# The head of a compression stage: small loads, a retention step, a bias product and a row copy in other places

## What is computed

```python
def _compress(kv_rows, pe_k, w1_k, w2_k, pe_v, w1_v, w2_v, k_norm_g):
    ...
    def phi(x, pe, w1, w2):
        x = (x + pe[:, None, :]).transpose(0, 1, 3, 2, 4).reshape(B, n_cmp, NSA_GROUPS, CMP_BLK * HEAD_DIM)
        return jax.nn.gelu(x @ w1) @ w2

    kc = _rms(phi(blk[:, :, :, 0], pe_k, w1_k, w2_k), k_norm_g)
    vc = phi(blk[:, :, :, 1], pe_v, w1_v, w2_v)
...
def _ret_chunk(R, q, k, v):
    ...
    o = o + jnp.einsum('bnhd,bhde->bnhe', q, R) * xi[None, :, :, None]
    R = jnp.exp(C * lg)[None, :, None, None] * R + jnp.einsum('bmhd,bmhe->bhde', k * zeta[None, :, :, None], v)
    return o, R
...
        return win[:, QS:]            # the window of the sample: its old rows, moved up by 4, and the new ones
```

## Time and profile before

| | us |
|---|---|
| median of 3 runs | 2939.29 (2936.84 to 2944.8) |
| the profiled execution, its own time | 2942.77 |
| its span in the trace | 2941.1 |
| projection, until the barrier | 0 to 435.2 |
| TensorE in the compression | 435.3 to 670.7 |
| prompt's attention begins | 673.9 |
| first expert's product | 1400.2 |

### The profile page before, as it was taken

How to read it: one execution, slowest core, us unless ns; L and a number is a source line. 1 busy time by engine, 2 the same in 40 slices (tenths; PEclk the granted TensorE clock), 3 DMA queues, 4 the chain that set the end, 5 groups by cost and what they waited for, 6 DMA issues and landing times.

```text
span 2941.1 us, 44519 instructions
## 1 busy us (share of the span) xinstructions
PE 2695.6 (92%) x18178; PEld 2223.1 (76%) x18178; DVE 945.1 (32%) x2675; ACT 636.7 (22%) x1613; POOL 484.7 (16%) x465
## 2 busy tenths in 40 slices
PE   7999976998998758993999999999999999999995
PEld 3555435545665557451999999999999999999994
DVE  1222222216766412345222232323232232223221
ACT  1111211115765400121011111111111111111111
POOL 0000011101000000022032131313132232122221
PEclk9999985998999856996999999999999999999997
DMA  5000036203000121222778788888898999999995
GB/s 187 11 22 20 23 116 142 58 1 113 2 1 1 58 86 58 94 81 95 284 231 275 260 263 275 278 291 292 308 302 303 331 320 308 331 315 312 317 327 166
DMA packets 276770, 533.64 MB, mean 181 GB/s; under 512 B 51906, under 2 KB 88226, under 8 KB 276354
## 3 DMA queue, kind: packets, MB, share of 16 engines
q1 hardware_dynamic: 223842, 472.66, 45.1%
q0 software_dynamic: 33312, 46.98, 7.5%
q10 hardware_dynamic: 19408, 11.10, 1.4%
HBM read 492.21 MB, written 42.96 MB: 182 GB/s over the span
## 4 chain that ended last, share of the span: by engine, by line
PE 51%; DMA 1%; DVE 1%; SPq 0%; POOL 0%; issue 0%; POOLq 0%; DVEq 0%; ACT 0%; ACTq 0%
PE up L2047 34%; PE down L2058 17%; DMA w_up<-summed_rows 1%; DMA slot_rows<-slot_tokens_gates 0%; DMA summed_rows<-y_rows,row_index_cur 0%; SPq L1995 0%; POOL summed_rows L2011 0%; PE down L2064 0%; POOLq L1891 0%; DVE nb L2179 0%; DVE hT L2136 0%; DVEq L1956 0%; DVE obt L2185 0%; DVE obt L2190 0%; DVE osf L2191 0%
## 5 line engine op out<-in xcount | busy, mean ns | idle before, releaser
L2047 PE MATMUL up<-hT,w_up 128*128 128x128 f32 (+19 forms) x8192 | 1006.6, 286 | 18.2 <-DVE hT L2136 18.2
L2047 PEld LDWEIGHTS up<-hT,w_up 128*128 128x128 f32 x8192 | 1003.5, 191 | 18.5 <-issue 18.5
L2058 PE MATMUL down<-actT,w_down 128*128 128x128 f32 (+19 forms) x4096 | 507.8, 286 | 0.0
L2058 PEld LDWEIGHTS down<-actT,w_down 128*128 128x128 f32 x4096 | 503.6, 191 | 1.1
L2011 POOL DMA_INDIRECT summed_rows<-y_rows,row_index_cur x153 | 240.9, 1574 | 1084.2 <-ACT y_rows L2077 1047.6
L2156 DVE TENSOR_SCALAR glu<-up,b_up_cur 128x128 f32<-128x128 f32 (+19 forms) x256 | 93.7, 366 | 1012.6 <-PE up L2047 1012.6
L306 PE MATMUL zp<-w_in,xnT 128*128 128x512 f32 (+3 forms) x896 | 355.7, 553 | 1.4 <-DVE xnT L476 1.4
L306 PEld LDWEIGHTS zp<-w_in,xnT 128*128 128x128 f32 (+1 forms) x896 | 153.5, 187 | 178.4 <-issue 174.6
L2088 ACT ACTIVATE sig<-glu 128x128 f32<-128x128 f32 (+19 forms) x256 | 82.4, 322 | 867.1 <-DVE glu L2156 867.1
L2096 ACT ACTIVATE yT<-down,b_down_cur 128x128 f32<-128x128 f32 (+19 forms) x256 | 97.0, 379 | 394.6 <-PE down L2058 394.6
L2005 POOL DMA_INDIRECT x_rows<-h_rows,row_index_cur x153 | 149.6, 977 | 65.2 <-issue 46.0
(11 more groups left out here) (395 smaller groups left out, 2070.6 us busy)
## 6 DMA issues: line engine op xcount, KB each, us to landing
w_up<-in_w_up SPq DMA_DIRECT2D x128, 2048.0 KB, 12.7
w_down<-in_w_down SPq DMA_DIRECT2D x64, 2048.0 KB, 12.6
w_in<-in_w_in SPq DMA_DIRECT2D x5, 2048.0 KB, 13.1
cache_rows<-in_cache_slc_kv SPq DMA_DIRECT2D x40, 128.0 KB, 2.5
x<-in_x_prompt SPq DMA_DIRECT2D x8, 512.0 KB, 3.8
window_rows<-in_cache_win_kv SPq DMA_DIRECT2D x8, 512.0 KB, 4.3
window_rows<-in_x_prompt SPq DMA_DIRECT2D x8, 512.0 KB, 4.0
summed_rows<-rg SPq DMA_DIRECT2D x8, 512.0 KB, 2.6
```

The lines of the kernel that those rows point to most:

```text
L2047: mm = nc.tensor.matmul(up[c % 2][:, h, :N], U[c // 4][:, h, kk, w0:w0 + P], hT[:, kk, :N], start=(kk == 0), stop=(kk == KC - 1))
L2058: mm = nc.tensor.matmul(dn[d % 2][:, :N], Dn[:, kk // 4, kk % 4, d * P:d * P + P], aT[:, kk, :N], start=(kk == 0), stop=(kk == KC - 1))
```

## The change

Seven edits in the head of the compression:
1. The two encodings and the gain are loaded by SyncE in the projection, in step t = 2, into `k.key` and `k.cnt`, which are free until the experts.
2. w1 of the values is loaded by ScalarE's queue behind its 16 pages of group 1 instead of at the start.
3. The copy of the old window rows goes from the projection to the end of SyncE's queue in the prompt's attention, behind the cache loads; `nout` of the sample tile is 3 instead of 4.
4. The retention's operands lie elsewhere (`x2T0` and the PSUM tiles `ctp1`, `ctp2`, `kcp`, `vcp`), and T(0,1) follows T(0,0) at once. `sample_operands()` stands on VectorE behind the first copy of M(0,0).
5. `retention()` stands on TensorE inside M(0,0), between the hidden halves hh = 0 and hh = 1. T(1,0) waits until its outputs have been copied from `ctp`.
6. The bias product takes one column of encodings, repeated 32 times, as the stationary operand and 256 columns of w1 as the moving one: 16 products, the step jj in column group jj % 4 (32 of 128 columns), so that the 16 steps leave four partial sums on 128 partitions.
7. VectorE copies these partial sums into `ret_sq`, and two products by a column of 1/32 (L796 after the change) add them up into the bias, behind the half hh = 0.

```diff
@@ phase_project
-        nout = lambda t: (4 if t == PT else 1 if t > PT else 3 if t >= 4 else 2)
+        nout = lambda t: (1 if t > PT else 3 if t >= 4 else 2)
             for t in range(NA):
+                if t == 2:
+                    with nc.allow_non_contiguous_dma(reason="position encodings and gain, small"):
+                        for j, n in enumerate(("k", "v")):
+                            sp.dma_start(k.pe_c[:, j, :], i[f"cmp_pe_{n}"][0].rearrange("(c r) d -> (r d) c", r=2)).then_inc(k.s_enc, 16)
+                        for half in range(2):
+                            sp.dma_start(k.gkc[64 * half:64 * half + 64, :], i["k_norm_cmp_g"].rearrange("l d -> d l")).then_inc(k.s_enc, 16)
...
-                    sp.dma_start(ws[:, :WIN - QS, :], i["cache_win_kv"].rearrange("l b s k g d -> (l b) s (k g d)")[:, QS:, :]).then_inc(so, 16)
@@ phase_compress, ScalarE
-                for j, n in enumerate(("k", "v")):
-                    act.dma_start(w1[j][:], i[f"cmp_w1_{n}"][0].rearrange("(c p) h -> p c h", p=P)).then_inc(s_w[j], 16)
-                    act.dma_start(pe_c[:, j, :], i[f"cmp_pe_{n}"][0].rearrange("(c r) d -> (r d) c", r=2)).then_inc(s_w[j], 16)
-                for half in range(2):
-                    act.dma_start(gkc[64 * half:64 * half + 64, :], i["k_norm_cmp_g"].rearrange("l d -> d l")).then_inc(s_s, 16)
+            act.dma_start(w1[0][:], i["cmp_w1_k"][0].rearrange("(c p) h -> p c h", p=P)).then_inc(s_w[0], 16)
...
                 if (op, gi, kv) == ("T", 0, 1):
                     load_pages(act, 1, ACT_PAGES, s_xa)
+                    act.dma_start(w1[1][:], i["cmp_w1_v"][0].rearrange("(c p) h -> p c h", p=P)).then_inc(s_w[1], 16)
@@ phase_compress, TensorE
+                    if (gi, kv) == (1, 0):
+                        pe.wait_ge(s_rc, 1)
...
-                    if (gi, kv) == (0, 0):
-                        retention()
                 if op == "M":
                     if gi == 0:
-                        pe.wait_ge(s_w[kv], 32)
-                        if kv == 0:
-                            pe.wait_ge(s_st, 1)
-                        for hh in range(2):
-                            for jj in range(16):
-                                mm = nc.tensor.matmul(bp[:, 2 * kv + hh:2 * kv + hh + 1], w1[kv][:, jj, hh * P:hh * P + P],
-                                                      pe_c[:, kv, jj:jj + 1], start=(jj == 0), stop=(jj == 15))
+                        pe.wait_ge(s_w[kv], 16)
+                        pe.wait_ge(k.s_enc, 64)
+                        if kv:
+                            pe.wait_ge(s_be, 1)
+                        for jj in range(16):
+                            q = 32 * (jj % 4)
+                            mm = nc.tensor.matmul(bp[q:q + 32, HID * kv:HID * kv + HID], pe_c[:, kv, jj:jj + 1].broadcast_to([P, 32]),
+                                                  w1[kv][:, jj, :], start=jj < 4, stop=jj >= 12)
...
+                        if gi == 0 and hh == 0:
+                            pe.wait_ge(s_bp, kv + 1)
+                            for part in range(2):
+                                mm = nc.tensor.matmul(bp[:, HID * kv + part:HID * kv + part + 1], sq_r[:, part * P:part * P + P], share[:],
+                                                      start=True, stop=True)
+                            mm.then_inc(s_b, 1)
+                            if kv == 0:
+                                retention()
@@ phase_compress, VectorE
-            sample_operands()
...
-                if (op, gi, kv) == ("M", 0, 0):
-                    sample_state()
...
                 if op == "M" and gi == 0:
-                    dve.wait_ge(s_b, kv + 1)
-                    nc.vector.tensor_copy(bias[:, 2 * kv:2 * kv + 2], bp[:, 2 * kv:2 * kv + 2]).then_inc(s_be, 1)
+                    dve.wait_ge(s_b, 2 * kv + 1)
+                    nc.vector.tensor_copy(sq_r[:], bp[:, HID * kv:HID * kv + HID]).then_inc(s_bp, 1)
+                    if kv == 0:
+                        sample_operands()
+                    dve.wait_ge(s_b, 2 * kv + 2)
+                    nc.vector.tensor_copy(bias[:, 2 * kv:2 * kv + 2], bp[:, HID * kv:HID * kv + 2]).then_inc(s_be, 1)
+                    if kv == 0:
+                        sample_state()
@@ phase_prompt, SyncE
             load_caches(sp, k, 0, False)
-            sp.wait_ge(s_out, 16 * 7)
+            sp.dma_start(o["win_s"].rearrange("l b s k g d -> (l b) s (k g d)")[:, :WIN - QS, :],
+                         i["cache_win_kv"].rearrange("l b s k g d -> (l b) s (k g d)")[:, QS:, :]).then_inc(s_out, 16)
+            sp.wait_ge(s_out, 16 * 7 + 16)
```

More of the change, by code:

```diff
@@ L611, in phase_compress @@
         ret_d = [kcp, vcp]
+        ret_s = [t[:SR, 0:2 * SR].rearrange("p (i n) -> p i n", i=2) for t in ret_d]
+        s_bp, s_rc = sem("pe_bias_parts_copied"), sem("s_ret_out_copied")
         first_t, first_m, nt_, nm_ = {}, {}, 0, 0
@@ L728, in retention @@
                 pe.wait_ge(s_rm, 1)
+                for e in range(2):
+                    pe.wait_ge(s_te[e], done_by(3, e))
                 for h in range(4):
```

44 lines of the change are left out of this document (24 added, 20 removed).

## The result

| | before | changed |
|---|---|---|
| median of 4 runs each, us | 2938.85 (2936.84 to 2944.8) | 2907.95 (2905.37 to 2912.02) |
| span of the profiled execution | 2941.1 | 2910.3 |
| last product of the projection over x (L306, now L311) begins | 414.06 | 414.35 |
| M(1,0) begins | 538.26 | 508.36 |

The ratio is 0.9893, with a 95% interval of 0.9874 to 0.9912: faster, by 31 us. The forecast was 2911 (2902 to 2924).

The account below looks back on a forecast made before the run. Barriers pass time cut from the compression's head to the end; there the chain through `ret_gain` and gates ends last. M(1,0) at 509.7 instead of 538.26 saves 28.5 us: 2942.8 becomes 2914.3, median 3.5 lower, 2911 us (2902 to 2924).

Parts of the forecast that it names:

- Old-row copy, -5.4: Projection's end: ScalarE's copy-out begins at 424.15 instead of 429.54, saving 5.4 us; the moved copy costs nothing under prompt attention.
- Small loads, nothing: Projection: encodings and gain take at most 36.9 us of SyncE's queue, x(4) still arrives in time, so no cost.
- T(0,0) at 445.4: Compression's head: ScalarE's freed queue copies at once, so T(0,0) to T(0,1) run from 445.4 to 449.4.
- Bias, 3.5 us: Bias product on TensorE: four column groups run side by side at clock 0.50, 3.5 us, range 3.5 to 13.9.
- `ret_gain` at 479.4, gates over at 484.8: Head, the chain ending last: SyncE's pages, then `ret_gain` at 479.4 (475.4 to 481.4), then VectorE's gates, 5.4 us.
- T(1,0) and S, 5.4 us behind the gates: Behind the gates: T(1,0) and S(0,0) take 4.4 us plus 1 for a fallen clock, ending at 490.2.
- M(0,1) with its sum, 8.6: Values' product: 11 slow and 53 fast instructions, 8.0 us, plus 0.6 for the sum, ending at 502.3.
- Rival A: Bias product stays in series or the clock stays low: saving only 18 us, 2921 us; chance 0.2.
- Rival B: SyncE's queue clears at once, `ret_gain` at 475.4, clock not fallen: saving 35 us, 2904 us; chance 0.15.
- Rival C: Traffic, not order, limits: w1 of the values lands at 501.6, saving 17 us, 2922 us; chance 0.1.
- Rival D: Small loads stop SyncE's queue in the projection for good, x(4) comes late, kernel slower; chance 0.03.

Follow-up runs that it names:

- run 1: Kernel before with only the old-row copy moved behind the cache loads of the prompt's attention: 2933.11 us, ratio 0.998, head 117.4 us.
- run 2: Kernel before with only the small loads (encodings and gain) moved into the projection: 2945.37 us, ratio 1.0018, head 130.8 us.
- run 3: Kernel before with the small loads in the projection and w1 of the values behind ScalarE's pages: 2938.88 us, ratio 0.9997, head 123.0 us.
- run 6: Changed kernel with w1 of the values back at the start of ScalarE's queue, behind w1 of the keys: 2918.68 us, ratio 0.9922, head 102.1 us.
- run 10: Changed kernel with w1 of the keys issued one line later, behind the sigmoids; in effect a repetition: 2914.26 us, ratio 0.9911, head 94.0 us.
- run 9: Changed kernel with the retention's gain loaded in the projection and the gates first on VectorE: 2906.3 us, ratio 0.9883, head 87.1 us.
- run 4: Changed kernel with the old bias product (64 one-column instructions, no sum by 1/32): 2918.25 us, ratio 0.993, head 104.8 us.
- run 12: Changed kernel with gain in projection, gates first, pages spread to GpSimd, retention behind both halves, w1 of the keys behind the sigmoids: 2900.09 us, ratio 0.9866.

## Why the prediction was right, point by point

The chain of steps was the one forecast, and the saving too: 29.9 us up to M(1,0) against 28.5 forecast, 30.8 in the span. M(1,0) came 1.3 us earlier than forecast, and that is a sum of errors of both signs: the gates 0.9 late, T(1,0) and S 0.1 longer, the bias 1.6 and M(0,1) 0.7 shorter.

- **Old-row copy, -5.4.** Right in kind, a little small: the copy-out begins right behind TensorE's products, and the compression's first load is issued 6.2 us earlier behind the last product over x than before (429.34 less 414.35, against 435.27 less 414.06). Run 1 gives 6.8 in the head. The old-row copy was issued at 676.85; only SyncE waited for it, at the end of its list, for 22.7 us under TensorE's attention.
- **Small loads, nothing.** Right in the sum, but the edit hides something that I hadn't weighed. The loads took 3.81 us of SyncE's queue, not up to 36.9. But I took their going from ScalarE's queue to be harmless in itself; alone it costs 6.6 us (run 2), and only edit 2 makes it harmless (runs 3 and 6).
- **T(0,0) at 445.4:** 446.41, 1.0 later. I had left the stretch from the compression's first load to T(0,0) as it was, 15.5 us; it is 17.1 (446.41 less 429.34), and 16.8 in run 3, which also has the small loads out of ScalarE's queue, against 15.1 in run 1, which doesn't.
- **Bias, 3.5 us:** 1.93. This is the mis-sized term. Four column groups do run side by side; but I put the clock at 0.50 behind the transposes, and it was at 1.00 from 450 on. 32 instructions of 217 ns, four at a time, are 1.74 us. The first half took 3.84 instead of 6.9 for the same reason. At the keys neither is worth anything, since the retention waits for `tables_b` (461.37, forecast 461.3) and ends as forecast (473.77, forecast 473.6); at the values 1.6 us are. The 1.93 at the keys is no constant either: the same product took 2.94 us in run 10.
- **`ret_gain` at 479.4, gates over at 484.8:** 480.39 (the row where the gates start) and 485.70. That it is so close is in part luck: SyncE's pages began 2.0 us later than the forecast's clock has them (447.46 against 450.85 less 5.4) and were issued in 28.26 us, 1.4 less than I had put. The gates are what T(1,0) waits for, and run 9, which takes them away, gives 6.9 us. I had not said what is next behind them: the last pages. T(1,0)'s transposes began at 479.74, not at the end of the second half (478.9), and in run 9 at 479.11.
- **T(1,0) and S, 5.4 us behind the gates:** 5.5 (485.70 to 491.17).
- **M(0,1) with its sum, 8.6:** 7.9 (493.03 to 500.89), warm from the start.
- **Rival A** did not come true: the groups ran side by side and the clock rose. Its price of 10.6 us is close to what run 4 measures (10.3 in the median, 10.8 in the head), but run 4 puts back the old product of one column, not the new one in series, and the agreement is luck in part: A had half of the price at each place and some of it back in M(0,1); measured, all of it stands at the values, and M(0,1) is longer.
- **Rival B** asked for an earlier queue; the pages took 28.26 us of it, where I had put a third of 6 off 31.67. **Rival C:** w1 of the values landed well ahead of need (its DMA took 10.4 us from issue to landing). Its second part, `ret_gain` at 481.4 with nothing gained in issue time, was 1 us too late. **Rival D:** the small loads did not stop SyncE's queue.

The 30.2 us of head, set down part by part: w1 of the values and small loads together 1.2 (run 3, from the kernel before), the copy 6.8 (run 1, from the kernel before), the bias 10.8 (run 4, back from the changed kernel), and 11.4 are left. These runs start from different kernels, so the list holds only as far as the parts add up. The 11.4 are a difference and were not run by themselves. By the rows they are T(0,1) no longer behind the retention and `tables_b`, which takes edits 4 and 5 and also edit 1, without which ScalarE's copies come too late; what each of these is worth stays open.

## What to carry to other kernels

Ask of each queue's load what size its packets are and what stands beside it: a queue of small packets gets one for one against a queue of large ones, so a big load in 1 KB packets belongs behind the small-packet loads that someone waits for. Before moving a small load out of a queue, look at what it was holding back. When a chain is shortened, take the last waiter's own wait apart (here gates behind a gain of 32 KB, 6.9 us of head in run 9), and look what waits next behind it (here the pages). And compare stretches of the trace that have a fixed start and end: medians of kernels with the same head stood 6 us apart.

## What the runs showed of the hardware

- In the changed kernel the clock rose about the 3.36 us of transposes: 0.59 from 446 to 450 and 1.00 right behind. The place isn't fixed: in run 10, with the same instructions, it was 0.50 in the transposes and 0.64 in the bias behind them, and in run 4, with products of one column behind them, 0.50 from 449 to 463.
- In the retention, whose products use 32 or 64 rows of the array, the clock was at 0.50 for 11 us of unbroken work, behind 5.62 us of idle time. With dense products directly ahead it ran at 1.00 in run 4 for the first 6 us, and at 0.98 through all of it in run 12 (16 instructions of this product, L739 in the changed kernel, in 1.08 us instead of 1.91). Whether the idle time or the small products keep it low, no run shows.
- Four groups of 32 columns ran side by side: 32 instructions with 256 moving columns in 1.93 us, where 217 ns each in series would be 6.9.
- A 32 KB load that spreads one row of 256 bytes over 128 partitions and was issued beside the first loads of the head went with 0.14 MB moved by both hardware queues in 2.5 us instead of 0.50.
- A DMA that stands behind an activation in ScalarE's list was issued 1.2 us before that activation began (432.37 and 433.57 in run 10; 429.17 and 430.38 in run 12). So the order of an engine's list, as told at the start, did not hold back this load.
